# A two-block transformer kernel on one core: four weight conversions on ScalarE moved to other steps of the recurrence stage

## The reference

```python
u = rmsnorm(h, norm_mix_w[l])
proj = u @ w_in[l]
hq, hf, hi, hg, att = jnp.split(proj, [...], axis=-1)
f = lb + (1.0 - lb) * jax.nn.sigmoid(hf)
log_f = jnp.log(f); k_hg = 1.0 - f; q_hg = hq * (HG_DK ** -0.5); v_hg = hi
# per chunk: b = cumsum(log_f); scores[t,s] = sum_k q[t,k] k[s,k] exp(b[t,k] - b[s,k]), s <= t
# out = scores @ v + (q * exp(b)) @ state
o_hg = rmsnorm(o_hg, hg_norm_w[l]) * jax.nn.silu(hg)
mix = jnp.concatenate([o_hg, o_att], axis=-1)
h = h + mix @ w_out[l]
```

## Time and profile before

| | |
|---|---|
| Median of 3 runs | 1261.67 us (1260.38 to 1264.94) |
| The profiled execution | 1264.94 us, span 1263.2 us |
| TensorE busy | 97% of the span |
| VectorE, GpSimd, ScalarE busy | 47%, 41%, 38% |
| Mean granted TensorE clock | 0.984 |
| Share of the DMA engines | 24.8% for the weights' queue |
| The recurrence stage | about 741 to 843 us of the span |

### The profile page before, as it was taken

How to read it: one execution, slowest core, us unless ns; L and a number is a source line. 1 busy time by engine, 2 the same in 40 slices (tenths; PEclk the granted TensorE clock), 3 DMA queues, 4 the chain that set the end, 5 groups by cost and what they waited for, 6 DMA issues and landing times.

```text
span 1263.2 us, 15300 instructions
## 1 busy us (share of the span) xinstructions
PE 1227.9 (97%) x5681; PEld 995.2 (79%) x5681; DVE 590.7 (47%) x846; ACT 480.9 (38%) x698; POOL 512.0 (41%) x289
## 2 busy tenths in 40 slices
PE   8999979999999999999999999999999999999997
PEld 6877737788888888888887778787888888888886
DVE  5686964235444445200174577973444444440003
ACT  6233634434333333222355554443343333332122
POOL 3631111254444344444474223226344444344442
PEclk9999987999999999999999999999999999999999
DMA  5330100123322223222213120112242323322221
GB/s 173 134 100 23 44 34 29 36 71 104 105 89 100 100 100 100 100 100 100 94 48 103 64 67 20 58 59 67 67 132 71 105 91 100 116 100 100 100 67 67
DMA packets 84598, 105.39 MB, mean 83 GB/s; under 512 B 2019, under 2 KB 77130, under 8 KB 84554
## 3 DMA queue, kind: packets, MB, share of 16 engines
q1 hardware_dynamic: 84394, 104.53, 24.8%
q10 hardware_dynamic: 160, 0.26, 0.1%
HBM read 102.43 MB, written 2.10 MB: 83 GB/s over the span
## 4 chain that ended last, share of the span: by engine, by line
PE 84%; DVE 5%; issue 4%; ACT 3%; POOL 3%; DMA 1%; SPq 0%; POOLq 0%; ACTq 0%; DVEq 0%
PE ps L1491 16%; PE ps L1493 16%; PE ps L1492 16%; PE ps L1793 9%; PE ps L1788 9%; PE ps L1575 4%; PE ps L1969 3%; POOL w_lo L427 2%; PE ps L1922 2%; DVE cy L1055 2%; PE ps L1617 1%; PE ps L1638 1%; DVE sp_lo L1090 1%; PE ps L1602 1%; PE ps L1592 1%
## 5 line engine op out<-in xcount | busy, mean ns | idle before, releaser
L427 POOL TENSOR_TENSOR w_lo<-w_raw,w_hi 128x1024 fp32r<-128x1024 f32 x180 | 433.4, 2411 | 616.5 <-ACT w_hi L550 615.3
L1491 PE MATMUL ps<-h_hi,w_hi 128*128 128x512 f32 x936 | 370.3, 396 | 2.1 <-DVE w_lo L983 1.4
L1493 PE MATMUL ps<-h_hi,w_lo 128*128 128x512 f32 x936 | 364.6, 390 | 0.0
L1492 PE MATMUL ps<-h_lo,w_hi 128*128 128x512 f32 x936 | 364.6, 390 | 0.0
L550 ACT ACTIVATE w_hi<-w_raw 128x1024 fp32r<-128x1024 f32 x190 | 200.0, 1055 | 325.4 <-PE ps L1493 145.4
L1491 PEld LDWEIGHTS ps<-h_hi,w_hi 128*128 128x128 f32 x936 | 175.8, 188 | 43.8 <-issue 6.1
L1493 PEld LDWEIGHTS ps<-h_hi,w_lo 128*128 128x128 f32 x936 | 175.7, 188 | 37.4
L1492 PEld LDWEIGHTS ps<-h_lo,w_hi 128*128 128x128 f32 x936 | 175.9, 188 | 35.1 <-issue 0.5
L1181 DVE TENSOR_TENSOR ps<-ps,rbs 128x512 f32<-128x512 f32 x88 | 61.5, 699 | 172.0 <-PE ps L1493 171.6
L727 ACT ACTIVATE cv<-ps,par 128x512 f32<-128x512 f32 x44 | 34.3, 779 | 183.8 <-DVE ps L1181 161.9
L1147 DVE TENSOR_TENSOR xT<-xT,ps 128x512 f32<-128x512 f32 x24 | 16.4, 685 | 154.9 <-PE ps L1793 106.7
(11 more groups left out here) (276 smaller groups left out, 1710.0 us busy)
## 6 DMA issues: line engine op xcount, KB each, us to landing
w_raw<-in_w_up SPq DMA_DIRECT2D x33, 1024.0 KB, 5.0
w_raw<-in_w_down SPq DMA_DIRECT2D x22, 1024.0 KB, 4.7
w_raw<-in_w_in SPq DMA_DIRECT2D x21, 1024.0 KB, 5.1
w_raw<-in_w_gate SPq DMA_DIRECT2D x11, 1024.0 KB, 5.2
w_raw<-in_w_out SPq DMA_DIRECT2D x8, 1024.0 KB, 4.8
xtok<-in_x SPq DMA_DIRECT2D x4, 512.0 KB, 5.2
out_dram<-obuf SPq DMA_DIRECT2D x8, 256.0 KB, 2.1
sq<-in_final_norm_w SPq DMA_DIRECT2D x1, 512.0 KB, 6.0
```

What stands on the lines that cost most here:

```text
L427: pool.tensor_tensor(unit_view(w_lo, at, down), unit_raw(at, down), unit_view(w_hi, at, down).bitcast(F32), ALU.subtract).then_inc(s_lo, 1)
L1491: pe.matmul(ps[:, bank, :], whi, hi, start=first, stop=False, skip_group_check=True)
L1492: pe.matmul(ps[:, bank, :], whi, lo, start=False, stop=False, skip_group_check=True)
L1493: mm = pe.matmul(ps[:, bank, :], wlo, hi, start=False, stop=last, skip_group_check=True)
```

## The change

The table `UNIT_LEAD` goes. The four gate units keep their steps (7, 9, 11 and 13). The conversions of units 116 to 119 stood at steps 16, 19, 25 and 29; they now follow directly behind the four `take`s, at steps 12, 17, 22 and 27, inside the loop's branch for `FILL`. Step 12 now lies between the conversions of units 114 and 115, so unit 116 is converted before unit 115. Nothing changes in the programs of the other engines.

```diff
-UNIT_LEAD = {7: U_IN2 + 18, 9: U_IN2 + 19, 11: U_IN2 + 20, 13: U_IN2 + 21,
-             16: U_OUT2, 19: U_OUT2 + 1, 25: U_OUT2 + 2, 29: U_OUT2 + 3}
+GATE_LEAD = (7, 9, 11, 13)
 OWN_REST = {9: U_IN2 + 18, 12: U_IN2 + 19, 16: U_IN2 + 20, 20: U_IN2 + 21,
             22: U_OUT2, 24: U_OUT2 + 1, 28: U_OUT2 + 2, 32: U_OUT2 + 3}
...
                     else:
                         take(14 + t, aq[:, t - 4, :], ps[:, t - 4, :])
-                if i in UNIT_LEAD:
-                    lead(UNIT_LEAD[i])
+                        lead(U_OUT2 + t - 4)
+                if i in GATE_LEAD:
+                    lead(U_IN2 + 18 + GATE_LEAD.index(i))
```

## The result

The changed kernel takes 1271.84 us (median of 6 runs, 1269.72 to 1273.02), the kernel before 1262.4 us in the same comparison (6 runs, 1260.38 to 1265.73). The ratio is 1.0066, 95% interval 1.0052 to 1.0080: about 8.3 us slower (0.0066 x 1262.4). (The two medians differ by 9.4 us. The ratio goes by all eleven executions of the changed kernel on record: their median is 1270.72 us, and 1270.72 / 1262.4 is 1.0066.) The profiled execution of the changed kernel took 1268.72 us, span 1267.0 us. It is the fastest of the eleven, while that of before lies above its median, so the spans alone (1267.0 against 1263.2) show less than the runs do. Two more comparisons with the same kernel gave 1.0052 (1.0030 to 1.0074) and 1.0067 (1.0045 to 1.0088); they are among the experiments.

A forecast was written before the change was run, and what follows sets the result against it. TensorE and VectorE were taken to run nearly without pause, chained at every step. Terms 3.6 + 0 + 0 + 0.4 + 1.2 = 5.2 us on 1261.67 gave 1266.9 us, with 8 in 10 between 1263.5 and 1269.5.

The forecast's parts named there:

- Part 1, the stall: ScalarE's step 12: unit 116's conversion waits for its DMA, delaying step 13's exponential and TensorE; 3.6 us, bounds 3.3 to 4.3.
- Part 2: ScalarE's step 16, which unit 116's conversion leaves: no gain on TensorE's path, with 0.6 us allowed in either direction.
- units 117 and 118: ScalarE's steps 17 and 22: conversions moved there find their DMA landed; both were counted as nothing.
- Part 4, unit 119: Conversion moved to step 27 delays step 28's exponential, GpSimd's inverse root, VectorE and level 29: 0.4 us, between 0 and 0.6.
- Part 5, the clock: TensorE behind its 3.8 us idle: the clock falls to the lower level, costing 1.2 us, bounds 0 and 1.7.
- a fall that lasts longer: Rival, matmuls behind the stall: clock stays low longer or falls again, 7.4 us in all, 1269.1 us; chance 0.15.
- The starting point: The kernel before was taken at 1261.67 us, the median of three runs, and the forecast loss was added to it.
- transfer is hidden: Rival: the DMA lands before ScalarE is at step 12's end, so no change, 1261.7 us; chance 0.06.
- faster: Rival: earlier conversions could release a waiting user; only 0.6 us, 1261.1 us; chance 0.02 of beyond 0.5% faster.
- Stall without a fall: Rival: TensorE is held up but its clock stays up, 4.0 us in all, 1265.7 us; chance 0.27.

## Why the prediction was wrong

The mechanism was right nearly to the row, and the total was too small: 5.2 us were forecast and 8.3 measured. The time lies above the range, and the kernel is slower by more than 0.5%, which had been given 0.23. The step that failed is the size of the clock's term.

- **Part 1, the stall: right.** Landing in 4.8 us, ScalarE's wait 3.1 us, level 13 late. Predicted 3.6 us, within 3.3 to 4.3; measured 3.70 us in the first profile, 3.8 with the clock held up, 3.96 at most. In the first profile GpSimd's product at 0.97 instead of 0.83 us explains the difference; the rest in the others is the landing, for ScalarE's wait was 3.18 and 3.34 us there instead of 3.09. With the DMA issued early it goes, but for 0.8 us.
- **Part 2, and units 117 and 118: right.** Nothing gained at the old places, nothing lost at the new ones.
- **Part 4, unit 119: right in its path**, 0.65 to 0.67 us instead of 0.4, just above the bound of 0.6. VectorE is held for as long as was worked out: L1007 begins 836.73 - 832.61 = 4.12 us behind the `take` of step 27, against 833.06 - 829.55 = 3.51. What failed is the 0.2 us taken off because L1007 had been long with its 1.16 us; it takes 1.22 us now.
- **Part 5, the clock: the step that failed.** That it falls was right, and shown by the matmuls put in the gap. Its size was not. The sum took 1.2 us of one fall, because part of the slow time might lie in the gap, and held 1.7 for the bound, since the one row of such a gap showed a mean clock of 0.57 over 4 us. Three profiles of the changed kernel show one short fall and two long ones: 1.6, 2.9 and 2.8 us of clock instead of 1.2. In the short one no part lay in the gap; in the long ones 0.6 and 0.9 us did, but the clock stayed low for 6.8 us. The case "a fall that lasts longer", 7.4 us in all, had only 0.15; the three stages are +6.0, +7.6 and +7.3 us. That the slow spell comes in one or in two lengths could have been asked of the trace of before as well, for it holds other low stretches than the one quoted (a mean clock of 0.50 from 170 to 174 us and 0.75 from 174 to 178, and 0.50 from 210 to 220).
- **The starting point.** The sum stood on 1261.67 us, a median of three. The kernel before came to 1262.4, 1263.47, 1264.46 and 1263.37 us in the later comparisons, each with more runs. That is 0.7 us of the miss in absolute time in the comparison that was forecast (1 to 3 us in the later ones), and none in the ratio.

Set right, the terms are 3.7 to 4.0 us for the stall, 0.7 for unit 119 and 1.6 or 2.8 to 2.9 for the clock, and give the 6.0 to 7.6 us of the stages, a ratio of 1.0047 to 1.0060. The mean of the three stages, 7.0 us or 1.0055, lies within all three intervals, but below two of the three ratios (1.0066, 1.0052, 1.0067; their mean is 1.0062, 7.8 us). With it, 1262.4 us would have come to 1269.4 us, just inside the forecast range; the 1271.84 us that put the result outside it are 2.4 us more, and they stand on a median of six. What is left over is less than the scatter: 7.0 us are within the 7.6 us, give or take 1.0 us, of all executions. Whether it is chance or comes from longer falls in executions that weren't profiled stays open. For longer falls speaks the mean granted clock, 0.9816 over the 24 executions of the changed kernel and 0.9842 over the 59 of before for which it is recorded: that is 3.3 us of TensorE's time, give or take 1.4 us, which is what the long fall takes away, though the falls ahead of the stage are in these means as well. A cost outside the stage is seen in none of the twelve profiles.

The rivals: "transfer is hidden" and "faster" have nothing for them. "Stall without a fall" was made by hand (15 or 10 matmuls), at +4.5 us; it came by itself in none of the three profiles of the changed kernel. The Trainium skill's rule ("TensorE: Matmul & The Clock Gate", section "HAM oscillation — how this bites in real kernels"), that a wait for a DMA between bursts lets the array start the next one cold, held for this stall in all three profiles and in that with unit 116 alone, with one difference: in the first profile of the changed kernel the next burst began at the full clock, and the fall came 0.4 us into it. The gaps of 1.79 and 0.67 us that the inserted matmuls left show no fall. The two gaps of the earlier trace rows, which the prediction set beside that rule, were waits for VectorE and GpSimd and not for a DMA.

## What to carry to other kernels

Moving a conversion forward on an idle engine moves it towards its DMA, and an in-order queue hands the wait to whatever is behind it: here a copy whose reader comes some 25 us later (VectorE's step 22, at 813.0 us in the trace of before) held an exponential that two engines needed at once, and TensorE behind them. Before such a move, look for the instruction that lets the DMA be issued, add the landing time, and compare it with the new place; here the same unit one exponential further back cost 0.64 us instead of 5.14. And price a stall of TensorE with the clock behind it, from several low stretches of the trace and not from one.

## What the runs showed of the hardware

- A pause of TensorE in this stage was followed by the lower clock at 2.75, 3.95, 4.04, 4.07 and 4.21 us, and not at 0.67, 1.01 and 1.79 us (one profile each). The low stretch was 3.4 us long (gaps of 2.75, 3.95 and 4.07 us) or 6.8 us (4.04 and 4.21 us); the length of the gap alone doesn't decide which. It began from 0.9 us ahead of the gap's end to 0.5 us behind it, and each microsecond of it behind the gap cost 0.47 us: 1.3 to 1.6 us, or 2.8 to 2.9 us.
- Adding 15 matmuls whose result nobody reads made the stage of the changed kernel 1.5 to 3.1 us shorter, by keeping the clock up. (The ratios, 1.0046 beside 1.0052 to 1.0067, point the same way, but their intervals overlap, so this is seen in the profiles alone.)
- Where VectorE and GpSimd start an operation on 128x256 nearly together, the later of the two was the slow one. VectorE's product of 790.85 us in the changed kernel took 0.42 us, and GpSimd's, 0.05 us behind it, 0.97 us; in the trace of before GpSimd's of 827.54 us took 0.73 us, and VectorE's exponents, 0.05 us behind it, 0.96 us instead of 0.41.
- The time from the start of the span to the same instruction varies by 5.4 us between executions of nearly the same work (769.2 to 774.7), while the 428 us behind the stage agree within 0.2 us. The start goes with the time at the lower clock ahead of it, 27.3 to 40.9 us (correlation 0.97). So most of the scatter between profiled executions arises ahead of the stage and goes with the clock, and two instructions near each other in one trace are the better ruler.
